# Gate products by one level of Strassen in a fused attention, retention and convolution layer

## The reference, cut to what matters

```python
h = rms_norm(x, norm_g)
u = h @ w_in                                   # 1024 x 8704
v_c, b_c, c_c, z_c, q, k, v, z_a, gate_logits = split(u)   # gate_logits: 2 x 1024 columns
y_c = b_c * causal_depthwise_conv(c_c * v_c, conv_w) * silu(z_c)
y_a = y_c @ w_conv_out
o   = sliding_window_attention(rms(q), rms(k), v, sinks) * silu(z_a)
y_b = o @ w_attn_out
g_a, g_b = split(sigmoid(gate_logits + gate_b))
out = x + (g_a * y_a + g_b * y_b) @ w_out
```

## Time and profile before

| | us |
|---|---|
| median of 3 runs | 835.53 (835.29 to 836.46) |
| profiled execution, its time | 836.85 |
| its span (first to last instruction) | 835.0 |
| PE busy | 827.7 (99%) |
| DVE busy | 560.7 (67%) |
| ACT busy | 274.2 (33%) |
| POOL busy | 177.1 (21%) |

### The profile page before, as it was taken

The page is one execution under the profiler, slowest core; times in us unless marked ns, Lnnn a source line. Parts: engine busy times, 40 slices in busy tenths (PEclk is TensorE's granted clock), DMA queues, the critical chain, the costliest instruction groups (busy, mean ns, idle before and its releaser), DMA issues.

```text
span 835.0 us, 10710 instructions
## 1 busy us (share of the span) xinstructions
PE 827.7 (99%) x3974; PEld 685.5 (82%) x3974; DVE 560.7 (67%) x1049; ACT 274.2 (33%) x627; POOL 177.1 (21%) x190
## 2 busy tenths in 40 slices
PE   8999999999999999999999999999999999999998
PEld 7787888888888888888888888888888888888876
DVE  4898778768973485786578887887652222354987
ACT  3464465632212234344444545440000000010250
POOL 3112111111112111121223533352221122211110
PEclk9999999999999999999999999999999999999999
DMA  7232211121153232223222222222333323335892
GB/s 235 76 102 76 76 51 51 51 68 59 51 178 99 77 95 82 71 80 92 86 77 75 77 77 76 77 76 88 91 99 100 101 85 92 100 102 171 200 281 104
DMA packets 104137, 81.60 MB, mean 98 GB/s; under 512 B 3421, under 2 KB 87446, under 8 KB 103830
## 3 DMA queue, kind: packets, MB, share of 16 engines
q1 hardware_dynamic: 102182, 74.62, 29.1%
q0 software_dynamic: 1344, 4.19, 2.7%
q10 hardware_dynamic: 560, 2.11, 0.7%
HBM read 76.72 MB, written 2.10 MB: 94 GB/s over the span
## 4 chain that ended last, share of the span: by engine, by line
PE 92%; ACT 2%; DVE 2%; DMA 1%; issue 1%; POOL 1%; ACTq 0%; DVEq 0%; POOLq 0%
PE proj L1467 25%; PE proj L1465 25%; PE proj L1466 25%; PE bank_t L1479 3%; PE bank_o L1551 2%; PE score L1536 1%; PE score L1537 1%; DMA w_raw<-in_w_out_dram 1%; PE proj L1685 1%; PE score L1626 1%; PE score L1625 1%; PE bank_o L1644 1%; PE score L1513 1%; PE bank_o L1645 1%; PE score L1499 1%
## 5 line engine op out<-in xcount | busy, mean ns | idle before, releaser
L987 DVE TENSOR_TENSOR w_lo<-w_raw,w_hi 128x1024 fp32r<-128x1024 f32 x126 | 156.4, 1242 | 149.9 <-POOL w_hi L629 147.3
L629 POOL TENSOR_SCALAR w_hi<-w_raw 128x1024 fp32r<-128x1024 f32 x120 | 135.5, 1129 | 518.9 <-DMA w_raw<-in_w_in_dram 391.7
L1465 PE MATMUL proj<-xt_hi,w_hi 128*128 128x512 f32 x512 | 203.0, 396 | 0.0
L1467 PE MATMUL proj<-xt_hi,w_lo 128*128 128x512 f32 x512 | 200.0, 391 | 0.0
L1466 PE MATMUL proj<-xt_lo,w_hi 128*128 128x512 f32 x512 | 199.7, 390 | 0.0
L1467 PEld LDWEIGHTS proj<-xt_hi,w_lo 128*128 128x128 f32 x512 | 96.1, 188 | 20.8
L1466 PEld LDWEIGHTS proj<-xt_lo,w_hi 128*128 128x128 f32 x512 | 96.3, 188 | 19.4
L1465 PEld LDWEIGHTS proj<-xt_hi,w_hi 128*128 128x128 f32 x512 | 96.2, 188 | 19.2
L1465 PE MATMUL proj<-w_hi,xt_hi 128*128 128x512 f32 x152 | 60.9, 401 | 0.3 <-ACT prob L761 0.3
L1467 PE MATMUL proj<-w_hi,xt_lo 128*128 128x512 f32 x152 | 59.6, 392 | 0.0
L1466 PE MATMUL proj<-w_lo,xt_hi 128*128 128x512 f32 x152 | 59.4, 391 | 0.0
(11 more groups left out here) (347 smaller groups left out, 1490.4 us busy)
## 6 DMA issues: line engine op xcount, KB each, us to landing
w_raw<-in_w_in_dram SPq DMA_DIRECT2D x96, 512.0 KB, 3.7
w_raw<-in_w_out_dram SPq DMA_DIRECT2D x14, 512.0 KB, 3.4
w_raw<-in_w_conv_out_dram SPq DMA_DIRECT2D x8, 512.0 KB, 3.7
w_raw<-in_w_attn_out_dram SPq DMA_DIRECT2D x8, 512.0 KB, 3.8
quads<-in_w_out_dram SPq DMA_DIRECT2D x4, 1024.0 KB, 9.4
x_in<-in_x_dram SPq DMA_DIRECT2D x4, 512.0 KB, 7.4
x<-in_x_dram ACTq DMA_DIRECT2D x1, 2048.0 KB, 8.6
quads<-in_w_out_dram POOLq DMA_DIRECT2D x2, 1024.0 KB, 9.5
```

The lines of the kernel that those rows point to most:

```text
L629: pool.tensor_scalar(w_hi[:, slot, :], w_raw[:, slot, :], 1.0, 1.0, ALU.mult, ALU.mult).then_inc(hi_done, 1)
L987: dve.tensor_tensor(lo, raw_piece(n), hi.bitcast(F32), ALU.subtract).then_inc(w_split, 1)
L1465: pe.matmul(out, left[0], right[0], start=first, stop=False)
L1467: return pe.matmul(out, left[1], right[0], start=False, stop=last)
```

## The change

**Order.** The gate tiles leave the piece stream. Pieces 88 to 95 are now y_b (unit U_AOUT, right operand o2), 96 to 103 y_a (U_COUT, right operand yc). ACT copies these tiles, halved, to `y_b` and `part`. Pieces 104 to 131 carry the gate products, 132 to 145 the final product (FINAL).

**Gate products.** The logits (tokens x 1024 in, 1024 out, per branch) are computed by one level of Strassen in Winograd's form: 7 products instead of 8, in `PAIRS` = 8 pairs of column tiles t and t + 4, alternating between the branches. One product is 4 chunks x 3 matmuls, with a 128 x 128 weight block as the stationary operand and 256 tokens streaming. A piece holds two products' weights, loaded by two transfers of 256 KB. The 56 products go round all eight PSUM banks; product x waits until product x - 8 has been read.

```diff
+            for x in range(PRODUCTS):
+                pair, i = divmod(x, 7)
+                n, h = GATES + x // 2, x % 2
+                product = GATE_ORDER[i]
+                if h == 0:
+                    wait_low(n)
...
+                elif (x - 8) % 7 == 0:
+                    pe.wait_ge(u_copied, (x - 8) // 7 + 1)
+                else:
+                    pe.wait_ge(combined, 7 * ((x - 8) // 7) + COMBINED[GATE_ORDER[(x - 8) % 7]])
+                if x < 7 and LEFT[product][0]:
+                    pe.wait_ge(sx_split, 4)
...
+                for k in range(4):
+                    last = products(gate_banks[x % 8][:, 0:256], [t[:, k, :] for t in w], [t[:, k, :] for t in left], k == 0, k == 3)
+                last.then_inc(piece_done if h else half_done, 1)
```

```diff
+            def gate_step(x):
+                pair, i = divmod(x, 7)
+                ended = pair // 2 - 1 if 0 < pair <= PAIRS and pair % 2 == 0 else None
+                if i == 0 and ended is not None:
+                    merged_low(ended, 0)
+                if pair < PAIRS and i:
+                    combine(pair, GATE_ORDER[i])
+                if i == 1 and 0 < pair <= PAIRS:
+                    gate(pair - 1, 1)
+                if i == 2 and ended is not None:
+                    merged_low(ended, 1)
+                if i == 3 and ended is not None:
+                    left_sums(ended)
+                if i == 5 and pair < PAIRS:
+                    gate(pair, 0)
+                for n in range(ROUNDED_BY_ACT, PIECES):
+                    if ROUND_AT[n] + 1 == x and not low_on_pool(n):
+                        split_piece(n)
```

**Weights.** From piece 104 the ring has eight slots (four more in the place of yc, free from piece 104 on). ACT rounds the pieces from 108 on; DVE subtracts for the even ones, POOL for the odd ones:

```diff
+ROUND_AT = {n: max(2 * (n - GATES) - 8, n - ROUNDED_BY_ACT + 2) for n in range(ROUNDED_BY_ACT, PIECES)}
+            def pool_low(n):
+                raw, hi, lo = ring(n)
+                pool.wait_ge(block_hi_done, n - ROUNDED_BY_ACT + 1)
+                pool.tensor_tensor(lo, raw, hi.bitcast(F32), ALU.subtract).then_inc(pool_split, 1)
```

**Sums of weight blocks.** They are made in a DRAM tensor `w_sums` (12 blocks of 512 x 512: four for each gate matrix, four for w_out). SP copies twelve blocks there, one behind each of the pieces 20 to 27 and 48 to 51. POOL issues twelve accumulating transfers, one every second piece from 81 to 103:

```diff
+            def copy_block(i):
+                t, group = divmod(i, GROUPS)
+                sp.dma_start(w_sums[4 * group + t], w_block(group, *((0, 0), (1, 1), (1, 1), (1, 0))[t])).then_inc(w_copied, 16)
+            def gather(i):
+                group, step = divmod(i, 4)
+                t = (0, 2, 1, 3)[step]
+                if i == 0:
+                    pool.wait_ge(w_copied, 16 * 4 * GROUPS)
+                if step >= 2:
+                    pool.wait_ge(w_gathered[group], 16 * step)
...
+                pool.dma_start(w_sums[4 * group + t], source, accum_op=ALU.add).then_inc(w_gathered[group], 16)
```

**XD.** ACT scales x1 by the row factors first (XS, four copies of 1024 columns), and the eight XD steps become plain transposes, three half pieces later:

```diff
-XD_HOOKS = (7, 8, 9, 10, 15, 16, 17, 18)
+XS_HOOKS = (7, 7, 8, 9)
+XD_HOOKS = (10, 11, 12, 13, 14, 15, 16, 18)
-                        last = pe.matmul(xd_banks[m % 3][:, s * P:(s + 1) * P], x1[:, s, m * P:(m + 1) * P],
-                                         diag[1][:, s * P:(s + 1) * P], start=True, stop=True)
+                        last = pe.transpose(xd_banks[m % 3][:, s * P:(s + 1) * P], xs[:, m, s * P:(s + 1) * P], ident[:])
```

More of the change, by code:

```diff
@@ L57, with low_on_pool, lows_before, slot_of @@
 U_CONV = 14
[L58 to L71, removed]
-PIECES = FINAL + 2 * len(LEFT)
[L75 to L80, removed]
+U_AOUT = U_CONV + KC
+U_COUT = U_AOUT + KC // 4
+UNITS = U_COUT + KC // 4
+GATES = 4 * UNITS
+(A11, A12, A22, S1, S2, S3, S4) = range(7)
+LEFT = [(0, 0, 0), (0, 4, 0), (0, 4, 256), (1, 4, 256), (1, 0, 0), (1, 0, 256), (1, 4, 0)]
+ORIGINAL = {A11: (0, 0), A12: (1, 0), S4: (1, 1)}
+SUM = {S1: 0, S2: 1, S3: 2, A22: 3}
+GATE_ORDER = [A11, A12, S2, S1, S4, S3, A22]
+GROUPS = 3
+PAIRS = 2 * KC // 2
+PRODUCTS = 7 * PAIRS
+FINAL = GATES + PRODUCTS // 2
+PIECES = FINAL + 2 * len(LEFT)
+RING = 2 * SLOTS
+BANK_OF = [0, 2, 1, 3, 0, 1, 2]
+ADDS = [1, 1, 1, 0, 4, 3, 1]
+COMBINED = {A11: 0, A12: 1, S2: 2, S1: 3, S4: 4, S3: 6, A22: 7}
+SX_AT = [(1, 1), (0, 0), (0, 1), (1, 0)]
+ROUNDED_BY_ACT = GATES + SLOTS
+ROUND_AT = {n: max(2 * (n - GATES) - 8, n - ROUNDED_BY_ACT + 2) for n in range(ROUNDED_BY_ACT, PIECES)}
+COPY_AT = [*range(4 * U_GA, 4 * U_O0), *range(4 * U_Z0, 4 * U_Z1)]
+SUM_AT = [GATES + 2 * i - 8 * GROUPS + 1 for i in range(4 * GROUPS)]
+def low_on_pool(n):
+    return ROUNDED_BY_ACT <= n and n % 2 == 1
+def lows_before(n, pool):
+    return sum(low_on_pool(m) == pool for m in range(n + 1))
+def slot_of(n):
+    return n % SLOTS if n < GATES else (n - GATES) % RING
+def landings(n):
+    return sum((2 if GATES <= m < FINAL else 1) * (slot_of(m) == slot_of(n)) for m in range(n + 1))
 def added(product, s, i=0):
@@ L101, in unit_columns @@
             (TRA, [("w_in_2", Z2 + 512 + P * j) for j in range(4)])][u]
-    if u < U_GATE_A:
+    if u < U_AOUT:
         t = u - U_CONV
         return TRA, [("w_in_2", c + P * t) for c in (CV, CC, CB, CZ)]
[L105 to L124, removed]
+    t = 4 * ((u - U_AOUT) % (KC // 4))
+    return TRA, [("w_attn_out_2" if u < U_COUT else "w_conv_out_2", P * (t + j)) for j in range(4)]
 UNIT = [unit_columns(u) for u in range(UNITS)]
@@ L176, in steps_after @@
     i = 2 * (n - 4 * U_KV) + half
+    out += [("XS", s) for s in range(ST) if XS_HOOKS[s] == i]
     if i in XD_HOOKS:
@@ L403, in split_parts, with quarter, left_of @@
-        def split_parts(n):
-            held = (w_hi2, w_lo2) if n >= FINAL and (n - FINAL) % (2 * SLOTS) >= SLOTS else (w_hi, w_lo)
-            return [t[:, n % SLOTS, :] for t in held]
+        u_of = [th2[:, i * 256:i * 256 + 256] for i in range(2)]
+        w_of = [acc[:, i * 256:i * 256 + 256] for i in range(2)]
+        v_of = [spare[:, i, 256:512] for i in range(2)]
+        def quarter(t, row, col):
+            return t[:, 4 * col:4 * col + 4, row * 256:row * 256 + 256]
+        def left_of(hi, lo, s_hi, s_lo, product):
+            source, chunk, token = LEFT[product]
+            return [t[:, chunk:chunk + 4, token:token + 256] for t in ((hi, lo), (s_hi, s_lo))[source]]
@@ L834, in _ @@
+                    if half == 1 and 4 * U_COUT + 2 <= n < 4 * U_COUT + 6:
+                        q = n - 4 * U_COUT - 2
+                        act.wait_ge(sx_summed, (4, 6, 8, 10)[q])
+                        act.activation(quarter(sx_hi, *SX_AT[q]), quarter(sx, *SX_AT[q]), ACT.Copy).then_inc(sx_hi_done, 1)
                     if (n, half) in ((4 * U_K + 3, 1), (4 * U_Q + 3, 1)):
@@ L1205, in add_blocks @@
                     add(0, x11, x11, p2)
+                elif product == A22:
+                    add(0, x21, x21, p4)
                 elif product == S2:
@@ L1660, in _ @@
             keep_busy(4)
-            for n in range(FINAL):
+            for n in range(GATES):
                 u, q = divmod(n, 4)
```

475 lines of the change are left out of this document (300 added, 175 removed).

## The result

The changed kernel takes 849.49 us (846.13 to 851.73, four runs) against 836.0 us of the kernel before on the same chip: a ratio of 1.0159, 95% interval 1.0144 to 1.0174. Forecast were 828.0 us, within 823.5 to 838.5. It is slower by 13.5 us, 11 us beyond the range. The profiled execution took 848.93 us with a span of 847.2.

A forecast was written before the change was run, and what follows sets the result against it. TensorE, busy 99% of the span, bounds the kernel. Gains of 7.2 (gates), 3.5 (XD) and 0.8 us (final product's start) less 4.0 of handover stall make 7.5 us less: 828.0 us, range 823.5 to 838.5.

The forecast's parts named there:

- Gate products: PE in the gate stage: 672 matmuls of 256 columns at 0.120 us replace 384 of 512 columns; gain 7.2 us.
- XD: Second norm's scaling moves from PE to ACT; eight PE steps fall from 0.89 to 0.45 us each; gain 3.5 us.
- DMA, "I take 0": Added DRAM copies, accumulating transfers and gate-stage weight loads stay hidden behind PE's work; cost 0 us.
- POOL's split, 1.6 us: POOL's two-input subtraction for a low part lasts 1.6 us, between bounds of 1.05 and 2.11.
- The collision, 0.45 us per split: Gate stage: POOL splits stop DVE's SBUF-only instructions, half a split on average, 0.8 us per pair; PE still sets the pace.
- The handover, 4.0 us: Start of the final product: PE stalls 2.2 us for A11's fourth merged chunk and 1.8 us at S1; bounds 0 and 13.5.
- POOL's splits hold DVE up: Rival, chance 0.25: POOL splits of 2.1 us or more delay DVE in gates and final product, 13.5 us stall; 837.5 us.
- The DRAM sums come late: Rival, chance 0.04: POOL stands at a gather, roundings wait behind it; three waits of 5 us, 843 us.

The follow-up runs named there:

- experiment 4: The kernel before with only the change's scaling of the second norm (four ACT copies, eight steps of plain transposes, three half pieces later): 834.68 us.
- experiment 9: The change with only its twelve accumulating transfers issued six pieces earlier, behind pieces 75 to 97; POOL keeps its 19 splits: 842.54 us.
- experiment 1: The change with DVE making the low part of every weight piece, POOL none from piece 108 on: 835.01 us.
- experiment 5: The change with DVE making all low parts and the twelve accumulating transfers issued six pieces earlier, behind pieces 75 to 97: 827.43 us.
- sixth experiment: The change with POOL's subtraction on 8 of 1024 columns (odd pieces' low part missing, result wrong) and accumulating transfers six pieces earlier: 826.22 us.
- experiment 2: The change with POOL's subtraction on 8 of 1024 columns; PE reads the high part for odd pieces' low part, result wrong: 831.41 us.
- experiment 7: The change with DVE making all low parts in the final product; POOL keeps its 12 splits in the gate stage: 839.36 us.
- experiment 10: The change with accumulating transfers six pieces earlier and each POOL split cut into two subtractions of 512 columns: 839.35 us.
- experiment 11: The change with accumulating transfers six pieces earlier and POOL's split replaced by a one-input instruction writing the raw piece (result wrong): 826.01 us.

## Why the prediction was wrong, step by step

**Gate products: right.** Gain predicted 7.2 us, measured 87.8 - 80.2 = 7.6, in the kernels where nothing stalls; starts 0.12 us apart.

**XD: right at PE, wrong in the sum.** Timeline of after, PE at the first step and ACT at the convolution's first tile:

```profile
311.28 0.60 PE L1717 MATMUL score<-ident,xs 128*128 128x128 f32 x4
311.64 0.48 PE L1669 MATMUL proj<-w_hi,yc_hi 128*128 128x512 f32 x1
311.95 0.40 PE L1670 MATMUL proj<-w_lo,yc_hi 128*128 128x512 f32 x1
...
409.69 0.60 ACT L909 ACTIVATE vt<-proj 128x512 f32<-128x512 f32 x1
```

The same tile in the trace of before:

```profile
413.44 0.60 ACT L801 ACTIVATE vt<-proj 128x512 f32<-128x512 f32 x1
```

A step costs 0.67 - 0.23 = 0.44 us (predicted 0.45), and the tile starts 3.75 us sooner. Of these, 0.15 are there before the first XD step (transposes at 272.62 against 272.77 us). By 545 us 1.75 are gone. The step that failed is the silent one, that a gain ahead of the attention stage passes through it; experiment 4 measures 1.8 us in place of 3.5.

**DMA, "I take 0": wrong, 7 us.** The change less experiment 9 is 7.0 us; experiment 1 less 5 is 7.6. The two differences are between whole kernels, one pair with POOL's splits and one without, so they hold whichever way the weights came late. I compared shares of whole stages, 0.85 and 0.62, and did not lay the end of one beside the start of the next: four slots come free at once when the gates begin, pieces 107 to 111 are all asked for then, and the last transfers of POOL run beside them.

**POOL's split, 1.6 us: wrong, 2.64.** It lies above my upper bound of 2.11, which was the longest of 120 one-input instructions and says nothing of two inputs. The Trainium skill (GPSIMD Engine Reference, section 3.1) leads to an estimate of 2.25 us; the shortest of the 19 took 2.34, so page and trace nearly agree, and the trace has up to 3.10. The four of the change that took over 3 us each start some 0.4 us behind a DVE split, as the one at 722.49 behind DVE's at 722.11.

**The collision, 0.45 us per split (0.8 per pair of tiles): wrong, 1.32.** With the measured length the prediction's formula gives 2.68 / 2 x 5.7 / 10.1 = 0.76 us; so the length alone does not explain it. The step that failed is the average: half a hold in 5.7 of 10.1 cases, as if the two engines met at random. They don't. POOL starts as soon as ACT has rounded, and what DVE has next at that moment is set by the two fixed sequences: the same holds come back after every seventh POOL split, 14 pieces on. Timeline of after, POOL and DVE, one meeting of each kind:

```profile
733.90 2.50 POOL L718 TENSOR_TENSOR w_lo<-w_raw,w_hi 128x1024 fp32r<-128x1024 f32 x1 [4.04 <-ACT w_hi L787]
734.17 2.78 DVE L1337 TENSOR_TENSOR part<-logit,part 128x512 f32<-128x512 f32 x1
...
772.02 0.42 DVE L1315 TENSOR_TENSOR logit<-spare,proj 128x256 f32<-128x256 f32 x1
```

The first loses 2.1 us of its 2.78 to POOL; the second, an addition from PSUM inside the POOL split of 770.83 to 773.86, loses nothing. In this trace the 12 POOL splits of the gate stage stretch DVE's instructions by 0 to 2.15 us, five of them by at most 0.3 and six by more than 1.6, 1.14 on average; the 7 of the final product by 1.9. The Trainium skill (SBUF — State Buffer, Who interferes with whom) has the rule of mutual exclusion, and the 19 POOL splits of after agree with it; the prediction quoted it and priced it too low. (Its sentence speaks of two inputs; of the two rows that it gave, the cast has only one.)

**The handover, 4.0 us: wrong, 12.1** (54.2 against the sixth experiment's 42.1). I had one POOL split of 1.6 us before A11 and five more before S1. In the trace two stretch DVE by 2.5 us ahead of the `m_lo` that PE waits for at 800.24, and three stand close together in front of four low parts, since POOL subtracts as soon as ACT has rounded, whatever DVE has to do. And no term of the sum had the clock, which adds 2.7 and 1.4 us behind the two long waits.

**The rival.** "POOL's splits hold DVE up" was the mechanism, priced at 13.5 us of stall over a kernel where nothing stalls, and measured at 16.3 (experiment 9 less 6; over the fifth, where DVE makes these splits itself, it is 15.1). With the late weights cured the change is at 842.5 us, 5 above its 837.5: 2.8 of price, 1.7 of XD's gain that did not arrive, and 0.5 that I can't name. "The DRAM sums come late" was right too. In the change it came as congestion at the start of the gates; in experiments 1, 2 and 7 POOL did stand at a transfer with a rounding behind it, for 7.2, 7.2 and 3.0 us, as that rival says. It was priced at three waits of 5 us and cost 7. I had given the two 0.29 together and made them exclude each other. That experiment 5 comes to 827.4 us, close to the forecast's 828.0, is luck: it makes no POOL split and waits 0.6 us where the forecast has 4.0 of stall, but it lacks 1.7 us of XD's gain, so that two misses nearly cancel.

In sum: the forecast of 828.0 us, 7.0 more for the late weights, 12.3 more for POOL's splits (16.3 in place of 4.0) and 1.7 for XD make 849.0 us, against 849.49.

## What to carry to other kernels

Work that moves from VectorE to GpSimd to relieve it can cost VectorE more than it saves: here some 1.3 us of hold for 1.14 us of work. Compare these two before anything else, and if GpSimd must help, give it one-input instructions short enough for the other's slack. Lay transfers out by the moment at which slots come free, not by the mean share of a stage; and price a wait of several us on TensorE with the slower clock that can follow it.

## What the runs showed of the hardware that I had not expected

A POOL subtraction of 8 columns takes 0.53 us on average (experiment 6), one of 512 columns 1.58 (experiment 10) and one of 1024 2.34 to 3.43 us (the change and experiment 9). POOL's one-input instruction of 1024 columns stretches DVE's subtraction of 512 columns from 0.69 to 0.93 us on average (experiment 11, `s_lo`). In the change 1 MB from DRAM to DRAM took 7.2 to 7.4 us in the median, and the same with accumulation 9.7 to 10.1 us, beside other transfers. PE's granted clock was at its lower level behind the waits of 3.58, 2.92 and 1.85 us, but at the upper one, 1.00 from 780 to 793 us, behind that of 2.42 us. In experiment 9 a wait of the same 2.42 us, at 780.95, is followed by 3 us in which 256-column matmuls start 0.21 us apart in place of 0.12. No run here tells what decides it.
